# By-token products of 400 columns in layers 0 and 1 of a two-block transformer kernel

## What is computed

```python
mod_lat = silu_c @ w_ada[l] + b_ada[l]
mod_ctx = silu_cc @ w_ada[l] + b_ada[l]
...
sh, sc, gt = jnp.split(mod_lat, 3, axis=-1)
xn = _rms_norm(x, g_norm) * (1 + sc[:, None]) + sh[:, None]
cn = _rms_norm(ctx, g_norm) * (1 + sc_c) + sh_c
(au, av, az, bq, bk, bv, bz, cq, ck, cv, co, cz, cg) = _split_proj(xn @ w_in)
...
q_lat = _apply_rope(heads_q(bq), tabs)
k_lat = _apply_rope(heads_k(bk), tabs)
...
li_f, lf_f, li_b, lf_b = gates(cg)
...
h_lf, _ = _mlstm_scan(ql, kl, vl, li_f, lf_f, st_f, True)
...
x = x + gt[:, None] * (jnp.concatenate([y_a, y_b, y_c], axis=-1) @ w_out)
```

## Time and profile before

| | us |
|---|---|
| median of 3 runs | 1131.89 (1131.02 to 1132.49) |
| the profiled execution | 1129.82 |
| its span, first to last instruction | 1128.0 |
| TensorE busy | 1095.8 |
| VectorE busy | 720.7 |
| ScalarE busy | 591.8 |
| GpSimd busy | 136.5 |

### The profile page before, as it was taken

The page is one execution under the profiler, slowest core; times in us unless marked ns, Lnnn a source line. Parts: engine busy times, 40 slices in busy tenths (PEclk is TensorE's granted clock), DMA queues, the critical chain, the costliest instruction groups (busy, mean ns, idle before and its releaser), DMA issues.

```text
span 1128.0 us, 20227 instructions
## 1 busy us (share of the span) xinstructions
PE 1095.8 (97%) x8264; PEld 968.3 (86%) x8264; DVE 720.7 (64%) x1221; ACT 591.8 (52%) x970; POOL 136.5 (12%) x160
## 2 busy tenths in 40 slices
PE   8999999999999999899999999999999999999998
PEld 7787888766777989689898999999997799999997
DVE  5546567276535667766865686766676666776664
ACT  5332666444334557756565555544563646454454
POOL 0000010054020000423332100000014311000000
PEclk9999999999999999999999999999999999999999
DMA  9732212177421434035453455455452234545551
GB/s 373 308 112 76 75 38 75 40 278 279 151 75 38 150 130 141 1 121 189 150 178 113 153 188 221 153 184 200 174 187 78 103 122 144 196 182 187 189 192 49
DMA packets 25964, 169.07 MB, mean 150 GB/s; under 512 B 3344, under 2 KB 3728, under 8 KB 6288
## 3 DMA queue, kind: packets, MB, share of 16 engines
q1 hardware_dynamic: 24336, 165.67, 40.6%
q10 hardware_dynamic: 1536, 2.10, 0.7%
HBM read 164.62 MB, written 1.05 MB: 147 GB/s over the span
## 4 chain that ended last, share of the span: by engine, by line
PE 84%; DVE 6%; ACT 4%; DMA 2%; issue 2%; POOL 2%; SPq 0%; ACTq 0%; DVEq 0%; POOLq 0%
PE bank L425 24%; PE bank L426 23%; PE bank L427 23%; DVE wlo L419 2%; ACT whi L404 2%; PE bank L1521 2%; PE bank L471 1%; PE bank L1387 1%; DMA PROJ<-in_stream 1%; PE bank L1531 1%; PE bank L1541 1%; PE bank L1414 1%; PE bank L1405 1%; PE bank L1262 1%; DVE STAT L1564 1%
## 5 line engine op out<-in xcount | busy, mean ns | idle before, releaser
L425 PE MATMUL bank<-OPH,whi 128*128 128x256 f32 (+1 forms) x1716 | 524.1, 305 | 5.5 <-ACT AV L2774 2.2
L426 PE MATMUL bank<-OPL,whi 128*128 128x256 f32 (+1 forms) x1716 | 514.8, 300 | 0.0
L427 PE MATMUL bank<-OPH,wlo 128*128 128x256 f32 (+1 forms) x1716 | 514.8, 300 | 0.0
L419 DVE TENSOR_TENSOR wlo<-raw,whi 128x1024 fp32r<-128x1024 f32 x256 | 305.3, 1235 | 105.7 <-ACT whi L404 105.7
L425 PEld LDWEIGHTS bank<-OPH,whi 128*128 128x128 f32 x1716 | 328.0, 191 | 26.8 <-issue 9.5
L426 PEld LDWEIGHTS bank<-OPL,whi 128*128 128x128 f32 x1716 | 328.2, 191 | 12.0 <-issue 1.4
L427 PEld LDWEIGHTS bank<-OPH,wlo 128*128 128x128 f32 x1716 | 328.1, 191 | 10.9
L404 ACT ACTIVATE whi<-raw 128x1024 fp32r<-128x1024 f32 x256 | 255.7, 1049 | 100.7 <-PE bank L427 100.0
L425 PE MATMUL bank<-whi,OPH 128*128 128x256 f32 (+1 forms) x272 | 89.2, 328 | 0.0
L426 PE MATMUL bank<-wlo,OPH 128*128 128x256 f32 (+1 forms) x272 | 87.2, 321 | 0.0
L427 PE MATMUL bank<-whi,OPL 128*128 128x256 f32 (+1 forms) x272 | 87.1, 320 | 0.0
(11 more groups left out here) (290 smaller groups left out, 1193.3 us busy)
## 6 DMA issues: line engine op xcount, KB each, us to landing
raw<-in_stream SPq DMA_DIRECT2D x147, 1024.0 KB, 4.8
PROJ<-in_stream SPq DMA_DIRECT2D x5, 1024.0 KB, 14.8
X<-in_x_in SPq DMA_DIRECT2D x4, 512.0 KB, 5.8
PROJ<-PROJ ACTq DMA_DIRECT2D x32, 64.0 KB, 4.1
C<-in_con SPq DMA_DIRECT2D x1, 1413.5 KB, 9.8
out<-PROJ SPq DMA_DIRECT2D x4, 256.0 KB, 2.0
WST<-in_w_s SPq DMA_DIRECT2D x2, 256.0 KB, 5.1
PROJ<-in_last_gain SPq DMA_DIRECT2D x1, 512.0 KB, 6.5
```

The lines of the kernel that those rows point to most:

```text
L419: nc.vector.tensor_tensor(c.w[1][:, part], c.raw[:, part], c.w[0][:, part].bitcast(F32), ALU.subtract).then_inc(*raises(c.lo[h]))
L425: nc.tensor.matmul(out, w[0], x[0], start=start, stop=False, skip_group_check=skip)
L426: nc.tensor.matmul(out, w[0], x[1], start=False, stop=False, skip_group_check=skip)
L427: return nc.tensor.matmul(out, w[1], x[0], start=False, stop=stop, skip_group_check=skip)
```

## The change

- **Head weights.** `bk` (128 columns), `cv` (256), `bv` (128) and the gates (16) become one matrix of 528 columns, sent as two chunks of 128 x 2112: `head0` with blocks 0 to 3 and `head1` with blocks 4 to 7. Each is split in halves of two blocks. The stream's rows are padded to 2112 floats. `GWH` and `GWL` go.
- **By-token products.** For each of four groups of 128 tokens one job multiplies 400 columns (`cv`, `bv`, gates). ScalarE copies them out in two instructions, to `VA` and to `VG`; VectorE adds the gate bias from there. `values_fm`, `gates_fm`, both turns and the two `cv` jobs go. `keys` stays a job of 512 tokens.
- **Opening.** Vectors, identity and the first four blocks of X are one transfer, the other four blocks a second (`FIRST`). The first four chunks in the order of loading are: first of pair 0, second of pair 0, `head0`, first of pair 1; `head1` comes behind pair 2. Five jobs (four groups of tokens, keys) are filled one block at a time between the modulation steps. The sum of squares moves behind the two multiplications of pair 0. Of 60 dummy products 42 stay. Scaling, split and low part of blocks 0 and 1 alternate on VectorE.
- **Order.** `ck_0` and `ck_1` follow the five jobs; `cumulate` stands between them, and `running_maxima` and `turn_keys` directly behind `ck_1`. `filled_together` in layer 1 takes the same five jobs and brings the split of one chunk more.
- **Turn of modulation rows.** Four transposes with the identity in place of the four matmuls, and a reduction on VectorE over the four groups ahead of the bias.
- **PairedSquares.** GpSimd adds the two halves (256 columns), and TensorE issues one matmul.
- **Keys.** `rotate_keys` multiplies 64 columns of the rotation matrix and of the identity twice, into partitions 0 to 63 and 64 to 127, in place of `duprot` and `dup`.

```diff
             def pe(e):
                 first = s.first
-                ck0, ck1, keys, values = first.jobs[0:4]
+                by_token, keys = first.jobs[0:TT], first.jobs[TT]
                 keep_clock(e, pairs[0].row.mem, 36, pairs[0].row.empty)
+                pairs[0].multiply(e, 0)
+                pairs[0].multiply(e, 1)
                 for point in due(e, tot.empty, ("ones_set",), ("squares_added",)):
                     e.wait_ge(*point)
                 nc.tensor.matmul(tot.mem[:], ONES[:], sq[-1].mem[:], start=True, stop=True).then_inc(
                     *raises(tot.full))
-                pairs[0].multiply(e, 0)
-                pairs[0].multiply(e, 1)
-                keep_clock(e, pairs[0].turned.mem, 4, pairs[0].turned.empty)
                 pairs[0].turn(e)
-                keep_clock(e, pairs[1].row.mem, 6, pairs[1].row.empty)
+                keep_clock(e, pairs[1].turned.mem, 6, pairs[1].turned.empty)
                 pairs[1].multiply(e, 0)
+                for j in (*by_token, keys):
+                    first.fill_part(e, j, (0,))
                 pairs[1].multiply(e, 1)
...
+            cv = [Job([(None, lambda m: m[:, 0:BY_TOKEN], KD,
+                        lambda k, tt=tt: (op(k, P * tt, P), head(k, P, BY_TOKEN)))], "act",
+                      lambda e, u, tt=tt: evict_tokens(e, u, tt)) for tt in range(TT)]
...
                 for j, src in enumerate((2, 3, 0, 1) if self.i < 4 else range(4)):
-                    mm = nc.tensor.matmul(self.turned.mem[:, 2 * j:2 * j + 2], self.room[:, P * src:P * (src + 1)],
-                                          con_("cond_rows"), start=True, stop=True, skip_group_check=True)
+                    mm = nc.tensor.transpose(self.turned.mem[:, P * j:P * (j + 1)], self.room[:, P * src:P * (src + 1)],
+                                             ident)
...
-                for h in range(2):
-                    mm = nc.tensor.matmul(self.tot.mem[:, 0:SEQ], ONES[:], self.sq[0].mem[:, h * SEQ:(h + 1) * SEQ],
-                                          start=h == 0, stop=h == 1)
-                mm.then_inc(*raises(self.full))
+                nc.tensor.matmul(self.tot.mem[:, 0:SEQ], ONES[:], self.sq[0].mem[:, 0:SEQ], start=True,
+                                 stop=True).then_inc(*raises(self.full))
...
+                    def twice(out, m, kv, x):
+                        for at in (0, 64):
+                            mm = nc.tensor.matmul(out[at:at + 64, :], m[:, 64 * kv:64 * kv + 64], x, start=True, stop=True)
+                        return mm
```

More of the change, by code:

```diff
@@ L32 @@
 CHUNK = 2048
+HEAD = 528
+WIDE = 4 * HEAD
+BY_TOKEN = 400
 EPS = 1e-6
@@ L249, with program @@
     pass
-def program(nc, known, stream, vecs, con, x_in, gate_w, gate_b, b_s, w_s, last_gain, out):
+def program(nc, known, stream, first, con, gate_b, b_s, w_s, last_gain, out):
     with ExitStack() as ctx:
@@ L576, in pe @@
                 pairs[1].multiply(e, 1)
-                keep_clock(e, pairs[1].turned.mem, 4, pairs[1].turned.empty)
+                for j in by_token[0:2]:
+                    first.fill_part(e, j, (1,))
                 pairs[1].turn(e)
-                keep_clock(e, pairs[2].row.mem, 10, pairs[2].row.empty)
-                for j in (ck0, ck1):
-                    first.fill_part(e, j, (0, 1))
+                for j in (*by_token[2:], keys):
+                    first.fill_part(e, j, (1,))
@@ L596, in pe @@
-                for j in (ck0, ck1, keys, values):
-                    first.fill_part(e, j, (6, 7))
+                for k in range(5, KD):
+                    for j in (*by_token, keys):
+                        first.fill_part(e, j, (k,))
             def act_operand(e, i):
@@ L983, in product @@
                         part[0].used = j.u.full
-            mine = [c for j in jobs for c, *_ in j.parts if c is not None]
+            heads = [j for j in jobs if j.head is not None]
+            if heads:
+                heads[-1].frees_head = True
+                heads[-1].head[0].used = ("head_half_used", heads[-1].head[0].i)
+                heads[-1].head[1].used = heads[-1].u.full
+            mine = [c for j in heads for c in j.head] + [c for j in jobs for c, *_ in j.parts if c is not None]
             first = mine[0]
@@ L1160, in projections @@
             s.keys = keys.u.freed
+            s.values = [k for j in cv for k in j.u.freed]
+            s.gates = [("gates_given", l)]
             s.q = [q[b if l == 0 else b // 2].u.freed for b in range(4)]
@@ L1211, in dve @@
                                             GB[:, l, :].unsqueeze(1).broadcast_to([P, TT, 16]),
-                                            ALU.add).then_inc(*raises(u.read["dve"]))
-                st.pe, st.dve = pe, dve
-                s.gates = u.freed
+                                            ALU.add).then_inc(*raises(("gates_given", l)))
+                st.dve = dve
             def filled_together(names):
                 jobs, st = [s.jobs[name] for name in names], stage(f"proj{l}_together")
+                ahead = jobs[0].head[1].s + 2
@@ L2902, in program @@
             if l == 0:
-                for name in ("ck_0", "ck_1", "keys", "values_fm"):
+                for name in ("cv_0", "cv_1", "cv_2", "cv_3"):
                     pr.emptied(name)
-                job("gates_fm")
-                rc.turn_keys()
-                job("cv_1")
-                pr.turn_gates()
+                pr.give_gates()
                 rc.log_forget()
-                pr.turn_values()
-                job("cv_0")
+                pr.emptied("keys")
+                job("ck_0")
                 rc.cumulate()
                 hn.square("k")
+                job("ck_1")
+                rc.running_maxima()
+                rc.turn_keys()
+                hn.scale("k")
                 job("q_0")
-                rc.running_maxima()
-                hn.scale("k")
-                job("q_1")
                 rc.carry_maxima()
                 rc.weigh_keys(0)
-                job("q_2")
+                job("q_1")
                 rc.row_maxima()
```

318 lines of the change are left out of this document (151 added, 167 removed).

## The result

The changed kernel took **1116.28 us** (median of four runs, 1113.32 to 1117.82); the kernel before, on the same chip and in the same session, 1132.19 (1131.02 to 1132.66). The medians differ by 15.9 us. The ratio on record is 0.9867, 95% interval 0.9851 to 0.9883, which is 15.1 us less, by the interval 13.2 to 16.9. The forecast was 1113.7, the range 1108.5 to 1120.5.

A forecast was written before the change was run, and what follows sets the result against it. TensorE, busy 97% of the span, was taken to bound the kernel. Terms -12.0 - 3.0 + 1.3 - 2.4 - 2.1 = -18.2 us gave 1111.6 from the profiled execution, 1113.7 for the median; range 1108.5 to 1120.5.

The forecast's parts named there:

- Products: By-token products of both layers: 400 columns at 0.180 us each, net -6.0 us per layer, -12.0 in all.
- Head of layer 0: Start through layer 0's key transposes: products -6.0, opening -3.0, wait for the copy of `ck` +0.65 us.
- the walk: Opening, step by step: first product at 21.9 us, waits for blocks 2, 4, 6 of 0.6, 0.2, 0.7.
- Rival 1: Opening gives nothing: idle TensorE drops to half clock, about 1.5 us, late blocks take the rest; 1116.7 us, chance 0.16.
- Behind the blocks: After the blocks, TensorE waits for ScalarE's copy of `ck_1` before `turn_keys`: +0.65 us per layer, +1.3 in all.
- Head of layer 1: Layer 1's products and key transposes: -6.0 us for the products, +0.65 for the copy of `ck`.
- Turns: Modulation-row turns beside layer 0's attention: 0.4 us saved each, six of eight counted, -2.4 us.
- Sums of squares: `PairedSquares.add`: one 256-column fp32 product less, half of 0.86 us, five times, -2.1 us.
- the multiplication by five: Sums of squares: the saving of half of 0.86 us counted in full at all five places, -2.1 us.
- Doubled keys: `rotate_keys`: eight products of 64 weight columns for four of 128, priced at 0, bounds 0 and +5.2 us.
- the 3 that the prediction allowed itself: TensorE waits behind the opening: prediction wrong if they, about 27 us in all before, grew by more than 3.
- One of its signs: Whole kernel: TensorE's busy time was to go down by about 15 to 17 us.

The follow-up runs named there:

- e2: Changed kernel with 12 dummy products put in front of the two transposes that turn the norm factor near 520 us; 1115.99 us.
- b1_turns: Kernel before with only the new turns of the modulation rows (four transposes, added reduction on VectorE); 1127.08 us against 1130.98, ratio 0.9965.
- e0: The changed kernel run once more, with nothing altered; 1115.54 us (1114.91 to 1116.93), ratio 0.986.

## Why the prediction came out as it did

**Products: right.** 400-column products stand 0.183 us apart:

```profile
347.51 0.34 PE L421 MATMUL bank<-whi,OPH 128*128 128x400 f32 x1
347.69 0.35 PE L422 MATMUL bank<-wlo,OPH 128*128 128x400 f32 x1
```

The forecast was 0.180. The straight line between the two measured widths was a good guide. The formula of the Trainium skill (TensorE: Matmul & The Clock Gate, Back-to-back issue gap) for isolated warm products gives 0.169 as an estimate; this trace doesn't agree, and it decides. The eight blocks of layer 1 take 23.10 us where the terms give 22.7: the 96 products account for 0.3 of that at 0.183 instead of 0.180, and the 24 products of `keys` for 0.1, at 0.232 instead of 0.227.

**Head of layer 0: right in sum, by luck; not in its parts.** The terms were -6.0, -3.0 and +0.65, together -8.35; the execution without a fall (`e2`) is 8.4 ahead at the attention, the profiled one 7.2. In the opening the first product came at 21.3 (forecast 21.9), but the waits for blocks 2, 4 and 6 were 0.84, 0.74 and 0.76, 2.3 together, where the walk had 0.6, 0.2 and 0.7. By the terms the blocks would end at 53.6 (the text said about 53); it was 54.4, so the opening gave about 2.2 of its 3.0, and some 1.0 where the clock fell. The rest came back from a wait that the prediction had left standing: 0.77 us for the weighed keys at 93.9 us of the kernel before is gone. Rival 1 had named the fall and priced it at 1.5; in the profiled execution it did happen and cost 1.24. It doesn't separate the two kernels' medians, since the runs of the kernel before also go down to a mean clock of 0.994. No run has the new opening or the by-token products alone; both terms are read from the whole change, aligned.

**Behind the blocks: right.** 0.65 per layer was forecast for the copy of `ck`:

```profile
68.16 1.06 PE L1823 MATMUL bank<-FIRST,PROJ 128*128 128x128 f32 x8 [0.62 <-ACT PROJ L1116]
...
363.00 1.06 PE L1823 MATMUL bank<-FIRST,PROJ 128*128 128x128 f32 x8 [0.67 <-ACT PROJ L1116]
```

**Head of layer 1: 0.8 short.** Forecast 5.35, measured 4.5. Besides the 0.4 of the blocks, two waits grew behind the shorter queue: for the weighed keys from 0.53 to 0.89, for the gates' inverse from 0.88 to 1.08. The prediction had said that this stretch has no slack; it looked at the stretch itself and not at the waits behind it.

**Turns: near, in part by luck.** 2.4 forecast, 2.1 measured, in `b1_turns` and in the whole change. A turn saves 0.35, not 0.4 (its four transposes take 0.53 from start to start, not 0.4). The waits of attention grew by 0.5 and were meant to grow by 0.8, and 0.2 went to the transposes behind the first turn.

**Sums of squares: wrong, the largest miss.** 2.1 forecast, 0.4 measured. In the prediction's sum the step that failed is the multiplication by five. It asked only whether GpSimd would be late and not what TensorE waits for next. Behind two of the sums stood a wait of 1.54 us, behind one a wait of 2.25, behind one a split of weights on VectorE, and those took the saved time back in full.

**Doubled keys: right.** 0 forecast, none measured.

Together: 8.4 + 4.5 + 2.1 + 0.4 = 15.4 us, and 15.6 to 16.4 at an equal clock, against 18.2. The profiled execution has 12.7: its fall in the opening took 1.24, and between 515 and 560 us the slow issues and the second fall took 1.5. The falls of the clock make the single execution anything from 1113.3 to 1117.8. The waits of TensorE behind the opening grew by 2.1 us, from 23.4 to 25.5, under the 3 that the prediction allowed itself. One of its signs missed: TensorE's busy time fell by 18.9 us, not by 15 to 17. The dummies of the opening, 17.1 us busy before and 11.2 now, have a part in that.

## What to carry over

A saved instruction pays only up to the next wait of its engine. Before a gain is multiplied by its count, look behind each place for the next wait and ask whether what it waits for has moved; an engine that is 97% busy still has places where the other engines set the time. A wait that a new order creates can sometimes be moved behind the next independent product, which here was worth 2.5 us. Compare executions at an equal granted clock, or aligned instruction by instruction, before explaining a difference of 3 us.

## What the hardware showed

- Falls of the granted clock come and go between executions of one kernel. An opening with 1.32 and 2.19 us of idle time kept the full clock (`e2`), one with 1.32 and 2.16 (`e0`) had half of it from 21.6 to 25.0 us, and the profiled one from 14.3 to 17.7. Dummy products in the gaps did not make the kernel faster: 1114.98, 1115.99 and 1117.19 us against 1115.54.
- The same two DMA issues by ScalarE took 1.25 to 1.27 us in six profiles and 1.66 to 2.35 in five others, and what stood behind them in its queue was late by as much. What makes them slow is open.
- A fall can be free: at 520 us in `e0_after_again` it filled what the next wait would have been, 0.2 us instead of 1.7.
